# Decoder-layer kernel: the third group's cache chunks issued from another queue, and finished heads handled one unit later

## The reference

```
h = rmsnorm(x); z = h @ w_in       -> u, v_A, q, k, v, gate_A, gate_B
a = gelu(u) * (tril(W_s) rmsnorm(gelu(v_A)) + b)
q, k = rotary(rmsnorm(q)), rotary(rmsnorm(k))      24 heads of 64, three groups of 8
b = sliding-window attention; groups (window, dilation) = (128,1), (512,4), (2048,16)
x += (sigmoid(gate_A) * (a @ w_oa) + sigmoid(gate_B) * (b @ w_ob)) @ w_o
x += relu(rmsnorm(x) @ w_ff1)^2 @ w_ff2
x += sigmoid(rmsnorm(x) @ w_ple_gate) * (p @ w_ple_proj)
```

## Time and profile before

| | |
|---|---|
| three timed runs | 1190.55 us median (1188.67 to 1191.53) |
| the profiled execution, its own time | 1194.56 us |
| its span, first to last instruction | 1193.0 us |
| mean granted clock of TensorE | 0.962 |
| PE matmul busy | 1088.8 us (91%) |
| DVE busy | 678.9 us (57%) |
| ACT busy | 414.9 us (35%) |
| POOL busy | 281.1 us (24%) |
| chain that ended last | PE 63%, DVE 11%, POOL 9%, SP issuing 6%, issue 5%, DMA 4%, ACT 2% |

### The profile page before, as it was taken

How to read it: one execution, slowest core, us unless ns; L and a number is a source line. 1 busy time by engine, 2 the same in 40 slices (tenths; PEclk the granted TensorE clock), 3 DMA queues, 4 the chain that set the end, 5 groups by cost and what they waited for, 6 DMA issues and landing times.

```text
span 1193.0 us, 21015 instructions
## 1 busy us (share of the span) xinstructions
PE 1088.8 (91%) x8470; PEld 1065.9 (89%) x8478; DVE 678.9 (57%) x815; ACT 414.9 (35%) x707; POOL 281.1 (24%) x411
## 2 busy tenths in 40 slices
PE   4888899799999889879488999999999999999997
PEld 4888889699999889879378998999999999999996
DVE  4347855576778775988473635444343444344553
ACT  4333244334432445423122546331231232143422
POOL 2786365604673001100000012011000101011300
PEclk9998989899999899889798999999999999999998
DMA  6535723577558743354456323546565655555422
GB/s 180 195 104 176 230 99 122 165 233 211 162 193 274 215 150 123 131 163 145 145 161 216 108 71 105 173 164 208 170 201 167 197 179 188 180 196 178 154 72 76
DMA packets 129921, 196.16 MB, mean 164 GB/s; under 512 B 28721, under 2 KB 104977, under 8 KB 128049
## 3 DMA queue, kind: packets, MB, share of 16 engines
q1 hardware_dynamic: 111888, 132.46, 35.1%
q0 software_dynamic: 3584, 54.14, 13.4%
q10 hardware_dynamic: 14368, 8.46, 2.4%
HBM read 186.07 MB, written 62.00 MB: 208 GB/s over the span
## 4 chain that ended last, share of the span: by engine, by line
PE 63%; DVE 11%; POOL 9%; SPq 6%; issue 5%; DMA 4%; ACT 2%; ACTq 0%; DVEq 0%; POOLq 0%
PE gm L1011 46%; SPq L473 6%; PE gm L987 3%; PE gm L988 3%; PE gm L989 3%; DMA w_raw<-in_w_in 3%; POOL st L1702 2%; DVE w_lo L1282 2%; DVE kv L1372 2%; POOL fin L1738 2%; POOL fin L1749 1%; PE psS L1158 1%; POOL rot L1748 1%; POOL rot L1746 1%; PE psS L1168 1%
## 5 line engine op out<-in xcount | busy, mean ns | idle before, releaser
L1011 PE MATMUL gm<-h_hi,w_hi 128*128 128x272 f32 x1088 | 233.2, 296 | 16.4 <-DVE w_lo L1282 10.4
L1282 DVE TENSOR_TENSOR w_lo<-w_raw,w_hi 128x1024 fp32r<-128x1024 f32 x150 | 178.8, 1231 | 102.8 <-ACT w_hi L588 101.2
L1011 PE MATMUL gm<-h_hi,w_lo 128*128 128x272 f32 x1088 | 229.1, 293 | 0.0
L1011 PE MATMUL gm<-h_lo,w_hi 128*128 128x272 f32 x1088 | 228.5, 292 | 0.0
L588 ACT CAST w_hi<-w_raw 128x1024 fp32r<-128x1024 f32 x150 | 150.4, 1047 | 168.1 <-PE gm L1011 116.5
L987 PE MATMUL gm<-w_hi,h_hi 128*128 128x256 f32 x640 | 193.1, 302 | 6.0 <-issue 6.0
L1011 PEld LDWEIGHTS gm<-h_hi,w_hi 128*128 128x128 f32 x1088 | 175.1, 193 | 18.1 <-issue 16.0
L988 PE MATMUL gm<-w_hi,h_lo 128*128 128x256 f32 x640 | 185.4, 290 | 0.0
L989 PE MATMUL gm<-w_lo,h_hi 128*128 128x256 f32 x640 | 184.4, 288 | 0.0
L1011 PEld LDWEIGHTS gm<-h_lo,w_hi 128*128 128x128 f32 x1088 | 175.1, 193 | 0.0
L1011 PEld LDWEIGHTS gm<-h_hi,w_lo 128*128 128x128 f32 x1088 | 174.0, 193 | 0.0
(11 more groups left out here) (245 smaller groups left out, 1456.5 us busy)
## 6 DMA issues: line engine op xcount, KB each, us to landing
w_raw<-in_w_ff SPq DMA_DIRECT2D x64, 512.0 KB, 5.2
out_kvs<-in_cache_kv_w POOLq DMA_DIRECT2D x64, 510.0 KB, 4.1
w_raw<-in_w_in SPq DMA_DIRECT2D x60, 512.0 KB, 6.2
kv<-in_cache_kv_w SPq DMA_DIRECT2D x128, 128.0 KB
kv<-in_cache_kv_w SPq DMA_DIRECT2D x64, 256.0 KB
out_kvs<-in_cache_kv_w POOLq DMA_DIRECT2D x32, 508.0 KB, 4.7
kv<-in_cache_kv_w SPq DMA_DIRECT2D x128, 64.0 KB
w_raw<-in_w_o SPq DMA_DIRECT2D x8, 512.0 KB, 4.6
```

The lines of the kernel that those rows point to most:

```text
L1011: last = nc.tensor.matmul(gm[:, 2 * b2 + half, 0:HALF], w, x[:, k0 + k, half * HALF:(half + 1) * HALF], start=first, stop=end)
L1282: vec.tensor_tensor(w_lo[:, r, cols], w_raw[:, hh], w_hi[:, r, cols].bitcast(F32), ALU.subtract).then_inc(w_lo_done, 1)
```

## The change

- The plan transposes the heads of q and k at slot s from unit s-3 (before: s-2).
- The two buffers of `fin` are used by full units alone (`finn` counts these); the heads of the 32 sample rows go to `Sn`, which also stages the sample rows of v, with a semaphore of its own, `rows_stored`.
- Keys are stored by ACT (`store_heads`) two slots after their unit, as soon as POOL has finished them, before their transposes.
- A slot of `sq` is free for ACT when POOL's first operation has read it (`sq_taken`).
- `load_queries(g)` stands at slot max(KEYS_END[g-1]+3, last q unit+6): 29 for group 1 (before: 25), 56 for group 2 (as before).
- The chunks of group 2 are issued by POOL, one slot after chunk n-5 is taken, on semaphores of their own (`late_landed`). The others stay with SP.
- The constants of the chunk mixer are loaded at slot 50 (before 47), their triangle is made at 52 (49), transposed at 53 (50), its rows are moved at 57 (54) and used at 60 (58). The four `bt` transposes stand at slot 77 (72).

```diff
+def full(u):
+    return UNITS[u][1] in ("k", "q") and UNITS[u][4] < 2
+def finn(u):
+    return sum(full(x) for x in range(u))
+def rown(u):
+    return sum(UNITS[x][1] in ("k", "q") and UNITS[x][4] == 2 for x in range(u))
...
-        if s >= 2 and UNITS[s - 2][1] in ("k", "q") and UNITS[s - 2][4] < 2:
-            order.append((s, ("qk", s - 2)))
+        if s >= 3 and full(s - 3):
+            order.append((s, ("qk", s - 3)))
...
-        if s == 50:
+        if s == 53:
             order.append((s, ("ws",)))
...
-        if s == 72:
+        if s == 77:
             order += [(s, ("bt", c)) for c in range(4)]
...
+        def landed(n):
+            return (late_landed if CHUNKS[n][1] == 2 else chunk_landed)[n % RING]
...
+        def wait_heads(engine, kind, g):
+            engine.wait_ge(rows_stored, 16 * (rown(UNIT[kind, (g, 1, 2)]) + 1))
...
                 for g in range(1, NG):
-                    if s == KEYS_END[g - 1] + 3:
+                    if s == max(KEYS_END[g - 1] + 3, UNIT["q", (g, 1, 2)] + 6):
                         load_queries(g)
                 for n in range(RING, NCH):
-                    if s == CH_SLOT[n - RING] + 3:
+                    if s == CH_SLOT[n - RING] + 3 and CHUNKS[n][1] < 2:
                         load_chunk(n)
...
                     if UNITS[prev][1] in ("k", "q"):
-                        act.wait_ge(fin_ready, kqn(prev) + 1)
+                        act.wait_ge(sq_taken, kqn(prev) + 1)
...
                     else:
+                        act.wait_ge(rows_stored, 16 * rown(u))
                         nc.scalar.copy(Sn[0:NS], gm[NS:2 * NS, u % 4, 0:256]).then_inc(lo_rows, 1)
...
+            def store_heads(u):
+                _, qk, g, i, sub = UNITS[u]
+                cols = slice(256 * i, 256 * i + 256)
+                act.wait_ge(fin_ready, kqn(u) + 1)
+                if sub == 2:
+                    dst = t[f"kvs{g}"][:, 0, WIN[g] - T:WIN[g], cols] if qk == "k" else q_rows[g, :, cols]
+                    act.dma_start(dst, Sn[0:NS]).then_inc(rows_stored, 16)
+                else:
+                    f, done = fin[:, finn(u) % 2], fin_stored[finn(u) % 2]
...
-                if n >= 2:
-                    prev = [x for x in range(u) if UNITS[x][1] in ("k", "q") and kqn(x) == n - 2][0]
-                    if UNITS[prev][4] < 2:
+                m = finn(u)
+                if sub == 2:
+                    if rown(u):
+                        pool.wait_ge(rows_stored, 16 * rown(u))
+                    f = Sn[0:NS]
+                else:
+                    if m >= 2:
+                        prev = [x for x in range(u) if full(x) and finn(x) == m - 2][0]
                         pool.wait_ge(t_ready, TINDEX[("qk", prev)] + 1)
-                    if fin_count(n - 2):
-                        pool.wait_ge(fin_stored[n % 2], fin_count(n - 2))
-                f = fin[0:rows, n % 2, 0:256 * nt]
+                        if fin_count(m - 2):
+                            pool.wait_ge(fin_stored[m % 2], fin_count(m - 2))
+                    f = fin[:, m % 2]
...
+            def load_chunk(n):
+                kind, g, j, nk = CHUNKS[n]
+                pool.wait_ge(keys_used if CHUNKS[n - RING][0] == "keys" else values_used, kind_count(n - RING))
+                if nk == 1 and kind == "keys":
+                    wait_heads(pool, "k", g)
+                if nk == 1 and kind == "values":
+                    pool.wait_ge(vn_stored[g], 16 * 2)
+                for dst, src in chunk_loads(n):
+                    pool.dma_start(dst, src).then_inc(late_landed[n % RING], 16)
...
+                for n in range(RING, NCH):
+                    if s == CH_SLOT[n - RING] + 1 and CHUNKS[n][1] == 2:
+                        load_chunk(n)
                 if s in COPY_AT:
                     pool.wait_ge(unit_ready, s)
                     copy_window(COPY_AT.index(s))
```

More of the change, by code:

```diff
@@ L87, in kqn @@
     return sum(1 for x in UNITS[:u] if x[1] in ("k", "q"))
+def full(u):
[4 more added lines that the diff above has]
+    return sum(UNITS[x][1] in ("k", "q") and UNITS[x][4] == 2 for x in range(u))
 def stores_heads(u):
     _, kind, g, _, sub = UNITS[u]
-    return sub == 2 or (kind == "k" and not (g == 0 and sub == 0))
+    return full(u) and kind == "k" and not (g == 0 and sub == 0)
 PIECES = [(0, h, b) for h in range(H) for b in range(2)] + [(1, h, 0) for h in range(H)] + [(2, h, 0) for h in range(H)]
@@ L340, in build @@
         lo_rows = sem("lo_rows")
-        fin_ready = sem("fin_ready")
+        fin_ready, sq_taken = sem("fin_ready"), sem("sq_taken")
+        rows_stored = sem("rows_stored")
         fin_stored = [sem("fin_stored0"), sem("fin_stored1")]
@@ L350, in build @@
         chunk_landed = [sem(f"chunk_landed{r}") for r in range(RING)]
+        late_landed = [sem(f"late_landed{r}") for r in range(RING)]
         q_landed, keys_used, values_used = sem("q_landed"), sem("keys_used"), sem("values_used")
@@ L425, in chunk_count @@
         def chunk_count(n):
-            return sum(16 * len(chunk_loads(x)) for x in range(n % RING, n + 1, RING))
+            return sum(16 * len(chunk_loads(x)) for x in range(n % RING, n + 1, RING) if (CHUNKS[x][1] == 2) == (CHUNKS[n][1] == 2))
+        def landed(n):
+            return (late_landed if CHUNKS[n][1] == 2 else chunk_landed)[n % RING]
         q_rows = nc.dram_tensor("q_rows", [NG, NS, 512], F32, kind="Internal").ap()
@@ L433, in build @@
         for u in range(U_FF):
-            if UNITS[u][1] in ("k", "q") and stores_heads(u):
-                FIN_STORES[kqn(u) % 2] += 16
+            if stores_heads(u):
+                FIN_STORES[finn(u) % 2] += 16
         def fin_count(n):
-            return sum(16 for u in range(U_FF) if UNITS[u][1] in ("k", "q") and stores_heads(u) and kqn(u) <= n and kqn(u) % 2 == n % 2)
+            return sum(16 for u in range(U_FF) if stores_heads(u) and finn(u) <= n and finn(u) % 2 == n % 2)
+        def wait_heads(engine, kind, g):
+            engine.wait_ge(rows_stored, 16 * (rown(UNIT[kind, (g, 1, 2)]) + 1))
         def x_bank(a, half):
@@ L473, in load_chunk @@
                     sp.dma_start(dst, src).then_inc(chunk_landed[n % RING], 16)
[L475 to L479, removed]
             def load_queries(g):
-                wait_heads("q", g)
+                wait_heads(sp, "q", g)
                 if g:
@@ L562, in _ @@
             sp.wait_ge(cache_copied, 16 * (64 + 32 + 16))
+            sp.wait_ge(rows_stored, 16 * rown(U_FF))
             sp.wait_ge(fin_stored[0], FIN_STORES[0])
@@ L784, in take_output @@
                 nc.scalar.copy(dst, psO[:, 0:W * n].rearrange("p (a d) -> p a d", d=W)).then_inc(o_out, 1)
[L786 to L790, removed]
+            def store_heads(u):
+                _, qk, g, i, sub = UNITS[u]
                 cols = slice(256 * i, 256 * i + 256)
-                dst = t[f"kvs{g}"][:, 0, WIN[g] - T:WIN[g], cols] if qk == "k" else q_rows[g, :, cols]
-                act.dma_start(dst, fin[0:NS, n % 2, 0:256]).then_inc(fin_stored[n % 2], 16)
+                act.wait_ge(fin_ready, kqn(u) + 1)
[4 more added lines that the diff above has]
+                    f, done = fin[:, finn(u) % 2], fin_stored[finn(u) % 2]
+                    if g == 0:
+                        act.dma_start(t["kvp0"][0, :, cols], f[:, 256:512]).then_inc(done, 16)
+                    else:
+                        dst = t[f"kvp{g}"][0, :, cols].rearrange("(b p) f -> p b f", p=128)[:, 2 * sub:2 * sub + 2]
+                        act.dma_start(dst, f.rearrange("p (a f) -> p a f", a=2)).then_inc(done, 16)
             def square_tile(a):
@@ L1091, in transposes @@
                     pe.wait_ge(fin_ready, kqn(u) + 1)
-                    f = fin[:, kqn(u) % 2]
+                    f = fin[:, finn(u) % 2]
                     for c in range(2):
@@ L1369, in take_keys @@
                 c = kv[:, n % RING, 0:nk]
-                dve.wait_ge(chunk_landed[n % RING], chunk_count(n))
+                dve.wait_ge(landed(n), chunk_count(n))
                 dve.wait_ge(q_landed, 16 * T * (g + 1))
```

35 lines of the change are left out of this document (13 added, 22 removed).

## The result

The changed kernel takes 1150.78 us median (1149.95 to 1155.11, four executions) against 1191.04 (1188.67 to 1191.57, four). The ratio is 0.9673, 95% interval 0.9645 to 0.9701, so 36 to 42 us faster, about 39. The forecast was 1145.5 with a range of 1129 to 1169. The profiled execution took 1155.11, its span 1153.7; before they were 1194.56 and 1193.0. Of all executions behind this document one, of the run e3, took 1806.27 us, at a mean granted clock of 0.656 where every other had 0.95 or more; it is in no median here.

The account below looks back on a forecast made before the run. PE bounds the kernel from 743 us on; before that it idles behind POOL in group 0 and SP's DMA queue. Gains 5.8 + 11.7 + 1.5 + 26 = 45.0 us against 1190.55 give 1145.5 us, range 1129 to 1169.

Parts of the forecast that it names:

- Term E: Late stretch, 505 to 630 us: third group's chunks issued by POOL instead of SP; gain 26 us, bounds 18.9 and 34.
- price p: Late stretch: POOL's time per DMA issue, taken as 0.485 us.
- rival two: Late stretch gives half, with a new PE wait at slot 78: Term E 13 us, time 1158.5; chance 0.17.
- Term B: Queries of group 1 at slot 29: SP does not stop, PE's 6.45 us wait and clock dip go; 11.7 us.
- Term A: Transposes a unit later, up to unit 22: PE gets one unit's work done inside its idle time; 5.8 us.
- Term C: Third group's q and k: the same one-unit lead, partly taken back by DVE; 1.5 us, bounds 0 and 5.3.
- early terms: Term A, Term B and Term C, the gains ahead of the late stretch; 19 us together.
- first rival: Early lead taken back where DVE is full or POOL becomes the bound; some 4 us stay, 1160.5; chance 0.20.
- Third rival: Late stretch: POOL's issue is dear; PE passes at 538.8 + 112p; at price p 1.2, 1215.5 us; chance 0.07.

Follow-up runs that it names:

- e3: Changed kernel with the sample rows of v staged in partitions 32 to 63, apart from the finished heads; 1144.43, 1150.74 and 1151.76 us, ratio 0.9639.
- e5: The changed kernel once more, unedited; 1152.24 us, ratio 0.9706.
- e2: Kernel before with only the third group's chunks issued by POOL, one slot after the use of chunk n-5; 1166.41 us, ratio 0.9811.
- e11: Changed kernel with four DVE copies of the chunk onto itself in each of the third group's nine key chunks; 1176.63 us, one execution.
- e7: Changed kernel with the queries of group 1 loaded at slot 25 again; 1159.43 us, ratio 0.9769.
- e4: Changed kernel with the q and k transposes planned from unit s-2 again, the rest kept; 1161.06 us, ratio 0.9758.
- e6: Same edit as e3 to the changed kernel, run again beside e5; 1148.75 us, ratio 0.9666.
- e12: Kernel before with one edit, the queries of group 1 loaded at slot 29; 1181.18 us, ratio 0.9905.

## Why the prediction was right, point by point

- **Term E** was 26 us; the trace has 27.2 between units 70 and 86 (29.7 in e5), and alone it is worth 22.5 by the ratio of e2. The mechanism is as argued: SP's jam delays weights. The stretch was to take DVE's 91.6 us and 5 of waits, 96.6; it takes 98. The price p was put at 0.485 and is 0.524. DVE sets the end, by its 93% and by e11. But POOL is as near: it issues without a pause for 66 us, though DVE waits for chunks only 2.1 us in all. The margin was smaller than the prediction said.
- **bt at slot 77** was counted as a risk (rival two). It is a gain of some 5 us at most. The 6.01 us ahead of it were late weights, as that rival's "against" said, and e2 shows it.
- **Term B** was 11.7 us and alone gives 11.3; beside the later transposes it gives 7.2 (e7). Panel 10's weights go out at 180.29 (the two DMAs of `w_raw` in SP's timeline there), before the 190 named.
- **Term A is the step that failed.** 4.9 of its 5.8 us are there at unit 15, by its mechanism (e4 has 0.2), and at unit 21 0.3 are left. What happens between is PE's 2.89 us by ACT's wait and 0.96 for ACT's probabilities, 3.9 of the 4.6. The prediction had both ways to lose it, as bounds and not as values: "Lower bound 0, if the first use of the lead is another wait", and "ACT now waits at the sample rows of v until the last head rows have landed ... bounded by 0 and by term A, which it would eat". It took A in full and the wait at nothing. e3 and e6 show that ACT's wait is not the only one: without it the wait for the probabilities takes 2.61 and 3.98 us.
- **Term C** (1.5, at most 5.3): the lead grows by 5.3 us from unit 33 to unit 53 (18.2). PE's 4.05 us by ACT's wait bring it to 14.0 at unit 54, and at unit 61 it is 12.3, behind a clock of 0.57 in the four us from 367 and waits for ACT and DVE.
- A and B also shared one wait. The 6.45 us of PE can be taken away once: either edit removes a good part of it (e4 9.6, e7 9.9, both 12.9 at unit 33). Adding them as if apart was an error in the sum.
- So the 19 us of early terms were 12.7 in the profile, of which e12 alone has all. The first rival was half right: a lead is taken back, but at ACT's waits (the store, then the probabilities) before DVE or POOL could do it. Sum by the profile: 12.7 - 0.5 + 27.2 = 39.4 against 45.0. The range held because the largest term was right; the early ones were not.
- **Third rival:** its price did not come, but the line that it gave for the time holds. Twice the DMAs turn the kernel to 1214.74; that its own case was 1215.5 is chance, since p is 1.1 and not 1.2. Its reason, an issue that waits for DVE, is seen under copies alone. The rule of the Trainium skill ("SBUF — State Buffer", section "SBUF: two separate sides") names copies as what locks POOL out, and e11's trace agrees: one issue per copy, at a pitch of 0.728 us. That is 1.4 times 0.524 and not the five times that the Trainium skill's example has; the copies here take only 0.694 us. Beside its multiplications and reductions, which are all that DVE does with the chunks, the pitch of 0.524 stays.
- What stays open: POOL's queue with the later slot, the size of the bt move, whether the v rows apart are worth their 3 to 4 us, and what ACT's probabilities wait for once the store is out of the way. One DMA for both positions of a load, which would halve POOL's issues, was not tried.

## What to carry to other kernels

When several engines wait in turn, look for the in-order DMA queue behind them, and ask of each issue what stands behind it: moving loads off the queue that carries the weights, and issuing them earlier, was worth 22 us; issuing them earlier in that same queue lost 22. When one edit buys a lead, look for the next waits that will spend it, in the same change first, and don't add two edits that cure the same wait. For many small loads count DMAs, not bytes.

## What the runs showed that was not expected

- POOL's price is per DMA: 0.524 us for 32 rows of 2 KB, 0.55 for 16 rows. The duration that the profile gives for one (1.13 us median) overstates it twofold, since consecutive ones overlap.
- A float32 copy of 128 x 1024 in SBUF takes DVE 0.694 us (2.88 for four), a multiplication or reduction of the same size 1.22; only the copies slowed POOL's issues, to one per copy.
- Two profiled executions of the same early code differ by 4.7 to 6.6 us in PE's progress between units 33 and 70 (before and e2). Those of the changed kernel and e5 differ by 1.5 us at unit 70 and by 4.0 at the end (39.4 and 43.4). The kernel before took 1184.25 to 1194.68 over all its executions.
